# Feed-forward norm of a two-block transformer kernel: rows turned unscaled by transposes, half of them inside the output projection, and the squared factor applied in the last addition

## The reference, cut to what matters

```
h  = x + merged @ w_out                      # output projection, 1024 x 1024
hn = h * rsqrt(mean(h*h) + 1e-6) * norm2_g   # norm in front of the feed-forward layer
a  = square(relu(hn @ w_ff1))                # 1024 x 4096
h  = h + a @ w_ff2                           # 4096 x 1024
out = rmsnorm(h, final_g)
```

## Time and profile before

| what | value |
|---|---|
| median of 3 runs | 771.52 us (771.48 to 771.83) |
| profiled execution, its own time | 771.5 us |
| its span, first to last instruction | 769.7 us |
| PE busy | 689.6 us (90%) |
| DVE busy | 357.2 us (46%) |
| ACT busy | 295.3 us (38%) |
| mean granted clock of PE | 0.972 |

### The profile page before, as it was taken

The page is one execution under the profiler, slowest core; times in us unless marked ns, Lnnn a source line. Parts: engine busy times, 40 slices in busy tenths (PEclk is TensorE's granted clock), DMA queues, the critical chain, the costliest instruction groups (busy, mean ns, idle before and its releaser), DMA issues.

```text
span 769.7 us, 13061 instructions
## 1 busy us (share of the span) xinstructions
PE 689.6 (90%) x5482; PEld 538.5 (70%) x5482; DVE 357.2 (46%) x571; ACT 295.3 (38%) x432; POOL 46.5 (6%) x84
## 2 busy tenths in 40 slices
PE   3999999899757677778999999999999999999996
PEld 3887778743323122224999989998889999999995
DVE  3568861521110110105946885535675645555443
ACT  4244430331111010005764544678255643444432
POOL 0000000000000000000073750000000000000000
PEclk9999999999999898889999999999999999999999
DMA  8999899999999999999845234314345356554001
GB/s 354 408 418 391 318 424 419 422 421 421 424 422 424 422 421 426 403 413 424 308 181 218 113 126 181 134 64 156 110 170 185 135 195 219 219 196 185 3 1 55
DMA packets 33038, 210.27 MB, mean 273 GB/s; under 512 B 4688, under 2 KB 5072, under 8 KB 8656
## 3 DMA queue, kind: packets, MB, share of 16 engines
q1 hardware_dynamic: 32976, 209.38, 68.3%
HBM read 208.32 MB, written 1.05 MB: 272 GB/s over the span
## 4 chain that ended last, share of the span: by engine, by line
PE 70%; DMA 16%; DVE 5%; SPq 3%; ACT 3%; issue 1%; DVEq 0%; ACTq 0%
PE psum L419 69%; DMA raw<-in_w_exp 12%; DMA raw<-in_w_in_t 3%; SPq L459 2%; SPq L474 1%; PE psum L427 1%; DVE wlo L512 1%; ACT whi L495 1%; DMA raw<-in_w_ada_q 1%; DVE XL L1962 0%; DVE X L2398 0%; DVE acc L534 0%; ACT G L1283 0%; DVE XT L1310 0%; ACT XT L2342 0%
## 5 line engine op out<-in xcount | busy, mean ns | idle before, releaser
L419 PE MATMUL psum<-XH,whi 128*128 128x256 f32 x736 | 210.2, 286 | 4.3 <-DVE XL L665 2.8
L419 PE MATMUL psum<-XH,wlo 128*128 128x256 f32 x736 | 208.3, 283 | 0.0
L419 PE MATMUL psum<-XL,whi 128*128 128x256 f32 x736 | 208.0, 283 | 0.0
L512 DVE TENSOR_TENSOR wlo<-raw,whi 128x2048 fp32r<-128x2048 f32 (+1 forms) x88 | 168.9, 1957 | 48.6 <-ACT whi L495 48.6
L495 ACT ACTIVATE whi<-raw 128x2048 fp32r<-128x2048 f32 (+1 forms) x79 | 139.4, 1802 | 38.9 <-PE psum L419 22.4
L419 PEld LDWEIGHTS psum<-XH,whi 128*128 128x128 f32 x736 | 139.2, 189 | 8.0 <-issue 3.5
L419 PEld LDWEIGHTS psum<-XH,wlo 128*128 128x128 f32 x736 | 138.8, 189 | 0.0
L419 PEld LDWEIGHTS psum<-XL,whi 128*128 128x128 f32 x736 | 138.6, 188 | 0.3
L419 PE MATMUL psum<-raw,G 128*32 128x512 f32 x456 | 67.7, 682 | 20.3 <-DMA raw<-in_w_exp 20.2
L419 PEld LDWEIGHTS psum<-raw,G 128*32 128x32 f32 x456 | 17.7, 123 | 57.5 <-issue 56.6
L1267 ACT ACTIVATE WT<-psum 128x256 f32<-128x256 f32 x8 | 3.1, 383 | 134.4 <-PE psum L419 98.6
(11 more groups left out here) (350 smaller groups left out, 947.1 us busy)
## 6 DMA issues: line engine op xcount, KB each, us to landing
raw<-in_w_exp SPq DMA_DIRECT2D x85, 1024.0 KB, 23.1
raw<-in_w_ff SPq DMA_DIRECT2D x32, 1024.0 KB, 5.3
raw<-in_w_in SPq DMA_DIRECT2D x22, 1024.0 KB, 6.5
raw<-in_w_ada SPq DMA_DIRECT2D x16, 1024.0 KB, 11.7
raw<-in_w_in_t SPq DMA_DIRECT2D x8, 1024.0 KB, 18.4
X<-in_w_exp SPq DMA_DIRECT2D x5, 1024.0 KB, 24.9
raw<-in_w_ada_q SPq DMA_DIRECT2D x4, 1024.0 KB, 17.3
raw<-in_w_out_t SPq DMA_DIRECT2D x4, 1024.0 KB, 9.8
```

The lines of the kernel that those rows point to most:

```text
L419: return e.matmul(o, l, r, start=start, stop=stop, skip_group_check=True)
L512: e.tensor_tensor(wlo[j % NS][:, x], ring[slot[i]][:, x], whi[j % NS][:, x], ALU.subtract).then_inc(*steps_(("lo", j, x.start // 1024), *[ ...
```

## The change

The rows are turned without a factor, by transposes (`turn`, a matmul in transpose mode against the identity), so nothing of the turning waits for r. The two banks q = 0 and 1, which hold the features of the first column half, are turned in `pe_hybrid` ahead of the last group (b,t) = (1,1) of the projection. Of the banks q = 2 and 3, tile 0 is turned behind that group and tile 1 after it, when the last addition to `X` is done. ACT's copies and DVE's scalar_tensor_tensors move with them: q = 0 and 1 in front of the last `x3` addition. The Exp has scale -1 in place of -0.5 and gives r*r (`rq`, step `x3_rq`). Each of the five last additions becomes a scalar_tensor_tensor, sum * rq + X. `hon`, its two DVE instructions and the step `x3_factor` are gone. The four banks are now 0 to 3 by name.

```
 act_hybrid:
-            for b, t in ((0, 0), (0, 1), (1, 0), (1, 1)):
-                ... square and sum, and for b = 1 Ln, Exp(scale=-0.5) -> rs, step x3_rs
+            for t in range(2):
+                act_x3(e, t, 0)
+            for q in range(2):
+                act_n4(e, q)
+            act_x3(e, 0, 1)
+            for q in range(2, 4):
+                act_n4(e, q)
+            act_pieces(e, 166)
+            act_x3(e, 1, 1)
+        def act_x3(e, t, b):        # as before, but
+                e.activation(rq[:, t:t + 1], rs[:, t:t + 1], ACT.Exp, scale=-1.0).then_inc(*hyb_act(("x3_rq", t)))
+        def act_n4(e, q):           # the two copies to XH of bank q, as before in act_ff
 dve_hybrid, behind the addition x3 of (t, b):
-                    if b:
-                        dve_factor(e, t)
+                    if b and not t:
+                        for q in range(2):
+                            dve_n4(e, q)
 pe_hybrid:
+            nb = Banks([0, 1, 2, 3])
...
+                        if k + b + t == 3:
+                            for q in range(2):
+                                pe_n4(e, nb, q)
...
+            for q in range(2, 4):
+                pe_n4(e, nb, q, (0,))
+            for q in range(2, 4):
+                pe_n4(e, nb, q, (1,))
+        def pe_n4(e, banks, q, ts=range(2)):
+            p = banks.take(e, ("n4", q)) if 0 in ts else bank(("n4", q))
+            for t in ts:
+                e.wait_ge(*at(("x3", t, q // 2)))
+                for c in (2 * q, 2 * q + 1):
+                    i = turn(e, p[:, 256 * (c % 2) + 128 * t:256 * (c % 2) + 128 * t + 128], X[:, t, 128 * c:128 * c + 128])
+            if 1 in ts:
+                i.then_inc(*ff_pe(("n4", "turned", q)))
 dve_ff:
-            for q in range(4):
+            for q in range(2, 4):
+                dve_n4(e, q)
 dve_sum:
-            e.tensor_tensor(X[:, t, cs], X[:, t, cs], p, ALU.add).then_inc(*ff_dve(("x4", t, part)))
+            e.wait_ge(*at(("x3_rq", t)))
+            e.scalar_tensor_tensor(out=X[:, t, cs], in0=p, scalar=rq[:, t:t + 1], in1=X[:, t, cs], op0=ALU.mult, op1=ALU.add).then_inc(
+                *ff_dve(("x4", t, part)))
 pe_ff:
-            (the 16 matmuls of X with hon)
```

More of the change, by code:

```diff
@@ L1862, in act_hybrid @@
             act_pieces(e, 164)
-            for b, t in ((0, 0), (0, 1), (1, 0), (1, 1)):
-                e.wait_ge(*at(("x3", t, b)))
-                e.activation(flat(XT[:, 4 * t + 2 * b:4 * t + 2 * b + 2, :]), X[:, t, 512 * b:512 * b + 512], ACT.Square,
-                             accum_out=(ss, ss2)[b][:, t:t + 1]).then_inc(*hyb_act(("x3_sq", t, b)))
-                if b:
[L1868 to L1872, removed]
+            for t in range(2):
[8 more added lines that the diff above has]
+        def act_x3(e, t, b):
+            e.wait_ge(*at(("x3", t, b)))
+            e.activation(flat(XT[:, 4 * t + 2 * b:4 * t + 2 * b + 2, :]), X[:, t, 512 * b:512 * b + 512], ACT.Square,
+                         accum_out=(ss, ss2)[b][:, t:t + 1]).then_inc(*hyb_act(("x3_sq", t, b)))
+            if b:
+                e.wait_ge(*hyb_act.last())
+                e.wait_ge(*at(("x3_bias", t)))
+                e.activation(rs[:, t:t + 1], ss2[:, t:t + 1], ACT.Ln, bias=sq2[:, t:t + 1], scale=1.0 / D).then_inc(*hyb_act())
+                e.wait_ge(*hyb_act.last())
+                e.activation(rq[:, t:t + 1], rs[:, t:t + 1], ACT.Exp, scale=-1.0).then_inc(*hyb_act(("x3_rq", t)))
+        def act_n4(e, q):
+            e.wait_ge(*at(("n4", "turned", q)))
+            for c in (2 * q, 2 * q + 1):
+                e.activation(XH[:, c, :], bank(("n4", q))[:, 256 * (c % 2):256 * (c % 2) + 256], ACT.Copy,
+                             scale=gcol[:, 3, c:c + 1]).then_inc(*ff_act(("n4", "H", c)))
         def act_z(e, h):
@@ L2091, in dve_weigh, with dve_n4 @@
             e.tensor_tensor(g, g, bank(("o_sb", n))[:, :], ALU.mult).then_inc(*hyb_dve(("read", ("o_sb", n)), ("weighed", n)))
-        def dve_factor(e, t):
-            e.wait_ge(*at(("x3_rs", t)))
-            e.tensor_scalar(hon[:, t, :], C["ident"], rs[:, t:t + 1], None, ALU.mult).then_inc(*hyb_dve(("x3_factor", t)))
+        def dve_n4(e, q):
+            for c in (2 * q, 2 * q + 1):
+                e.wait_ge(*at(("n4", "H", 2 * q + 1)))
+                e.scalar_tensor_tensor(out=XL[:, c, :], in0=bank(("n4", q))[:, 256 * (c % 2):256 * (c % 2) + 256],
+                                       scalar=gcol[:, 3, c:c + 1], in1=XH[:, c, :], op0=ALU.mult, op1=ALU.subtract).then_inc(
+                    *ff_dve(*[("n4", "ready", q), ("read", ("n4", q))] if c % 2 else []))
         def dve_z(e, h):
@@ L2403, in dve_bias, with pe_ff @@
                 *ff_dve(("last", "part" if t else "bias", t)))
[L2405 to L2414, removed]
+        def pe_ff(e):
             banks = Banks([4, 5, 6, 7])
@@ L2468, in tensor_engine @@
             pe_hybrid(e, banks)
-            pe_ff(e, banks)
+            pe_ff(e)
         def begin(counting_now):
```

## The result

The changed kernel takes 769.57 us (median of 10 runs, 768.21 to 770.31), the kernel before 771.63 us (10 runs, 771.24 to 772.19). The ratio is 0.997, 95% interval 0.9962 to 0.9978: 2.06 us or 0.3% faster. The profiled execution took 769.08 us with a span of 767.3; the one before took 771.5 with 769.7. The forecast was 769.1 and 767.3.

A forecast was written before the change was run, and what follows sets the result against it. The prediction took a serial chain through the norm, then PE alone from ff1's c = 6, to bound the kernel. From 771.5 us it took 2.61 off and added 0.24 for the last additions: 769.1 us, range 768.5 to 769.9.

The forecast's parts named there:

- The mark c = 6: ff1's first matmul on its third feature bank, after which PE alone sets time: 585.83 before, 583.22 forecast.
- given back: Rival: ff1's or ff2's weight pieces come no earlier, PE waits, only the additions' cost is left: 771.7 us; chance 0.04.
- Transposes ahead of the last group: Eight transposes before the projection's last 12 matmuls delay that group by 0.88 us, bounds 0.85 and 0.93.
- DVE's cover: DVE ends its four early XL at 578.9, 0.5 us before the last addition to X is due at 579.38.
- The rival in which the last addition waits: Early XL on DVE end 0.9 us later, so the last addition to X slips 0.4: 769.5 us; chance 0.08.
- The chain behind the last addition: Transposes, ACT copies and DVE XL, not PE, set when ff1 reaches c = 6: 2.61 us gained, bounds 1.9 and 3.1.
- M: Time from behind the projection's third group's last matmul to ff1's first c = 6 matmul: 10.25 us before, forecast 2.61 less.
- The stall at c = 4: In ff1, PE waits some 0.4 us for the second XL of the late banks.
- The additions: Last additions as scalar_tensor_tensor cost 0.06 us each; on the end's chain 0.24 us lost, bounds 0 and 0.5.
- ACT's later order: Weight pieces, then tile 1's square, Ln and Exp, run behind ACT's copies until 587.1, covered by PE: costs nothing.
- the rival in which it falls: PE's granted clock leaves 1.00 behind 579, ff1 loses 2.5 to 3 us: 771.9 us; chance 0.05.
- The sum: Whole kernel: 771.5 - 2.61 + 0.24 = 769.1 us, span 767.3; bounds 768.4 and 770.1.

The follow-up runs named there:

- e1: Kernel before with only its five last additions made scalar_tensor_tensor with a factor column of ones: 772.05 us, ratio 1.0.
- e4: Changed kernel with fp32 matmuls against the identity in place of the transposes, same places: 770.73 us, ratio 0.9981.
- e2: Changed kernel with plain additions at the end, leaving out the factor r*r and its wait: 769.04 us, ratio 0.9962.
- e3: Changed kernel with all sixteen transposes behind the projection's last group, copies and XL of all banks behind the last addition: 769.2 us, ratio 0.9962.
- e5: Changed kernel with tile 1's last square, Ln and Exp back in front of ACT's copies of banks 2 and 3: 769.97 us, ratio 0.9973.
- second batch: Changed kernel, unaltered, run again beside new runs of the kernel before: 769.59 us, ratio 0.9969.
- e7: Changed kernel with ff1's first round in halves, X divided by r*r on DVE, plain last additions and a new 128x2 tile: 771.05 us, ratio 0.9986.
- e10: As e7, but the new value lies in two columns of a tile already free, so no tile moves: 768.09 us, ratio 0.995.
- e8: Changed kernel with an unused 128x2 fp32 tile in front of sq2, moving later tiles by 8 bytes: 771.52 us, ratio 0.9996.

## Why the prediction was right, point by point

**The mark c = 6.** PE alone set the time from there. From that matmul to the second addition of tile 0 it is 172.14 us before and 172.16 after, and 172.18 and 172.13 in e1 and e4. The changed kernel again, e2, e3 and e5 have 171.87 to 171.92. The difference lies in ff1's first two rounds: from c = 6 to ff2's first matmul it is 20.94 to 20.96 us in the first four and 20.70 to 20.73 in the others, with matmuls 0.120 and 0.119 us apart. The changed kernel has both kinds, the kernel before and e1 only the longer, and why stays open. Nothing was given back: PE was busy without a gap to the end.

**Transposes ahead of the last group.** 0.88 was forecast. The group's last matmul started 578.81 - 575.41 = 3.40 after the slot against 2.49 before, 0.91 more.

**DVE's cover.** 0.5 us was forecast, 0.66 found. The rival in which the last addition waits did not happen.

**The chain behind the last addition.** M was forecast to shrink by 2.61 and shrank by 2.57. The terms I named stand: dropping the scaling matmuls' second record is worth 1.2 (e4), moving the square, Ln and Exp behind the copies 0.7 (e5). One is to be read differently. I listed "four of the eight copies and XL behind the last addition" among what goes and the 0.88 as a cost beside it. As a pair they are worth nothing (e3, M 7.56). The transposes inside the projection, which the title names, do not contribute; that the transposes need no factor does. The 1.2 and the 0.7 leave some 0.7 of the 2.57, which no run isolates. What is also gone is the wait for the factor and its diagonal matrix (DVE was idle for 1.35 us ahead of it, PE for 0.40).

**The stall at c = 4.** 0.4 us was forecast. Start to start it was 0.48 where the pace is 0.12, so 0.36.

**The additions.** 0.24 was forecast, 0.30 measured. The instructions are 749 and 483 ns and not 742 and 476, which makes it 0.26 (e1), and 0.04 come beside them, in part with the second wait. The prediction takes the second addition of tile 0 off the chain; that is the one at 757.97, and the one off the chain is the first (755.25). The count, three of 512 and one of 256, is right.

**ACT's later order.** It was put at nothing, and ACT waits for PE at the relu. The bank is free for longer than the two column groups (over 10 us) of the prediction: ff1 takes it again in its third round, at 614.96.

**The clock.** The granted clock stayed at 1.00, so the rival in which it falls did not happen. In the changed kernel, the stretches with the transposes and the waits:

```profile
576.00:579.00 3.00, 3.00 (x17) 2.50 (x15) 2.16 (x5) 2.68 (x8) 0.00 (x0) 1.00 0.75 240
579.00:582.00 3.00, 2.66 (x21) 2.23 (x19) 1.35 (x3) 1.54 (x5) 0.00 (x0) 1.00 0.58 221
582.00:585.00 3.00, 2.80 (x23) 2.72 (x23) 2.12 (x4) 3.00 (x3) 0.00 (x0) 1.00 0.21 63
```

**The sum.** 2.57 + 0.17 - 0.30 = 2.44, against a difference of the two profiled executions of 2.42. The difference of the medians is 2.06, and 2.40 in the second batch. The slot behind the third group lay at 575.41 and 576.66 in the two traces of the changed kernel, at 575.58 before, and at 575.30 to 576.62 in the others but e7's (578.80, in an execution 1.8 us above its median). So executions differ by over a microsecond ahead of the norm, in stages that the change doesn't touch, and 0.4 us between the two differences is less than that. That the profiled execution met the forecast to 0.02 us is luck in part: 0.17 of its gain lies ahead of the slot and is not the change's, without it the gain is 2.27 where 2.37 was forecast, and the median is 0.47 us above the forecast.

## What to carry to other kernels

Find the point from which one engine alone sets the time, measure from the last point that both kernels share to that one, and price a change by this distance: here the forecast for it was 2.61 and the trace has 2.57, where whole executions scatter by one to two microseconds. A factor for each row that commutes with what follows (relu, square) can leave a serial chain, and the cheap place to pay for it is an instruction that can carry it, here at 0.06 us each. Moving work ahead of a release only helps if the work doesn't itself delay the release: here eight transposes delayed it by 0.91 us and gained nothing. Try the version with all of it behind.

## What was not expected of the hardware

ff2's 512-wide matmuls took 396 ns in place of 389, 11.20 us in place of 10.92 a round, when the tiles behind one place moved by 8 or by 64 bytes; the projection's did the same (396 in place of 390). Most rounds of ff1 became a little shorter (11.39 us in place of 11.52). In this kernel the new small tile was best put where it moves no other (e10), and the cost of its place shows in a version that holds the tile and doesn't use it (e8).
